# Moving the tile rows of a two-block transformer kernel to follow the weight buffers in SBUF

## The chip, the core and the metric

The kernel runs on one core of one Trainium2 chip. The metric is the device time of one execution in microseconds. The kernel before was timed three times: 1530.94, 1524.48 and 1525.96 us, median 1525.96 us. A separate profiled execution took 1528.67 us, of which 1527.4 us lie between its first and its last instruction (its span).

## What is computed

Two blocks run one after the other on a sequence of 512 tokens of width 1024, all in float32.

```python
h = rms_norm(x, g_mix);  proj = h @ w_in          # first block: LRU branch, pooling branch, gates
x = x + (gates_a * (lru(proj) @ p_a) + gates_b * (pool(proj) @ p_b)) @ w_out
h = rms_norm(x, g_ffn)
x = x + (gelu(conv(h @ w_up)[:2816]) * conv(h @ w_up)[2816:]) @ w_down
# second block: modulation by c, SSM branch, top-k attention branch, gates, gated FFN
u = rms_norm(x) * (1 + scale1) + shift1;  z = u @ w_in_2
x = x + gate1 * ((sig(ga) * s5(z) + sig(gb) * dsa(z)) @ w_out_2)
x = x + gate2 * ((silu(u2 @ w_ffn_gate_2) * (u2 @ w_ffn_up_2)) @ w_ffn_down_2)
```

## The kernel before

Activations lie transposed: a tile is 128 channels (partitions) by S = 512 tokens, one row of 2048 bytes in each partition. Every dense product is made of 1976 blocks of 128 by 128 weights. `block` (L678) issues three matmuls of 512 columns per block: the rounded weights `whi` with the rounded activation ("hi"), the weights' rest `wlo` with "hi" (L687, L688), and `whi` with the activation's rest "lo" (L690). All three stream a tile row as the moving operand in the type float32r (the name `pl_r` in the profile); the weights are the stationary operand. That makes 3 x 1976 = 5928 such matmuls.

The weights come in units of eight blocks (4096 bytes per partition). SyncE's queue loads a unit into one of four `raw` buffers (L2375), ScalarE rounds it into one of four `whi` buffers (L1117) and writes its negative rounding into `wlo` (L1126), and a DMA from GpSimd's queue adds `raw` to that (L2259); eight units are done by VectorE instead (L2193). VectorE and ScalarE also evacuate the PSUM banks and make the "hi" and "lo" tiles (L1527, L1146 and others).

Buffers are placed once, by `Kit.__init__`. Named tensors are allocated one after the other from the first free byte of a partition, each rounded up to 32 bytes; after them `self.base` is rounded up to 32, and all other tiles are rows of 2048 bytes numbered from there. `layout` (L308) hands the row numbers out by a list of free rows, so which tile has which row number depends on the number of rows, `self.slots`, and on nothing else of the placement. `place` (L275) turns a row number into an address: `base + 2048 * i`, under two names, `pl_f` (float32) and `pl_r` (float32r).

The first free byte is 16481 and the end 229368. The kernel before has this placement in each partition (bytes; the last columns are the start's remainder):

| what | start | mod 2048 | mod 256 | mod 128 |
|---|---|---|---|---|
| `raw`, 4 x 4096 | 16512 | 128 | 128 | 0 |
| `whi`, 4 x 4096 | 32896 | 128 | 128 | 0 |
| `wlo`, 4 x 4096 | 49280 | 128 | 128 | 0 |
| `vec` (1936) | 65664 | 128 | 128 | 0 |
| `cst` (1536) | 67616 | 32 | 32 | 32 |
| `sml` (4244) | 69152 | 1568 | 32 | 32 |
| rows, 76 x 2048 | 73408 | 1728 | 192 | 64 |

(229368 - 73408) / 2048 gives 76 rows, and `layout` uses all of them.

`vec` holds the small parameter vectors, `cst` the identity, a tile of ones and a triangle, `sml` small columns that the kernel works out. Most operands of the vector work start at a row's start. Some don't: the pooling branch (L1653, L1656, L1658) works on parts of a four-row tile at 0, 2400 and 4800 bytes from its start; in the kernel before these parts start at 64, 32 and 0 modulo 128.

Of the kernel before, what the change touches and what calls it, by code (L numbers as in the profile page):

```python
# [12 lines left out]
S = 512  # L13
# [10 lines left out]
NEG = -3.0e38  # L24
BIG = 1.0e30
NBANK = 8

VECS = [
    ("g_mix", 8), ("b_gate", 16), ("conv_a_w", 40), ("conv_a_b", 10),
# [71 lines left out]
class Book:  # L101
# [5 lines left out]
    def __init__(self):  # L107
        self.events, self.gone, self.home, self.before, self.real = {}, {}, {}, {}, False
# [100 lines left out]
class Kit:  # L209


    def __init__(self, nc, top, x_d, w_d, mod_d, cond_d, vec_d, cst_d, inv_d, ssm_d, uk_d, spill_d,
                 tab_d, stk_d, xs_d, out_d):
        self.nc = nc
        self.x_d, self.w_d, self.mod_d, self.vec_d, self.cst_d, self.inv_d = (
            x_d, w_d, mod_d, vec_d, cst_d, inv_d)
        self.cond_d, self.xs_d, self.stk_d = cond_d, xs_d, stk_d
        self.ssm_d, self.uk_d, self.spill_d, self.tab_d, self.out_d = (
            ssm_d, uk_d, spill_d, tab_d, out_d)
        self.plan = []  # L220
        self.book = book = Book()
        self.at, self.freed = book.at, book.freed

        def sig(name, by=1):
            s = Sig(book, top.enter_context(nc.semaphore(name)), by)
            self.sigs.append(s)
            return s

        self.sigs = []

        self.pe_done, self.act_done = sig("pe_done"), sig("act_done")
        self.dve_done, self.pool_done = sig("dve_done"), sig("pool_done")

        self.w_hi, self.w_neg = sig("w_hi"), sig("w_neg")
        self.w_lo = [sig(f"w_lo{i}", 16) for i in range(NLO)]

        self.raw_in = [sig(f"raw_in{i}", 16) for i in range(NRAW)]
        self.mod_in = [sig(f"mod_in{i}", 16) for i in range(NMB + NMC)]
        self.x_out = [sig(f"x_out{i}", 16) for i in range(8)]
        self.x_in = [sig(f"x_in{i}", 16) for i in range(8)]  # L240
        self.cond_in = sig("cond_in", 16)
        self.vec_in, self.ident_in, self.tri_in, self.inv_in = (
            sig(n, 16) for n in ("vec_in", "ident_in", "tri_in", "inv_in"))
        self.ssm_in, self.uk_in, self.ki_in = (sig(n, 16) for n in ("ssm_in", "uk_in", "ki_in"))
        self.st_out = [sig(f"st_out{i}", 16) for i in range(4)]
        self.st_in = [sig(f"st_in{i}", 16) for i in range(4)]
        self.tab_out = {n: sig(f"{n}_out", 16) for n in TABS}
        self.tab_in = [sig(f"tab_in{q}", 16) for q in range(4)]
        self.gate_io = [sig(f"gate_io{i}", 16) for i in range(16)]
        self.y_out = [sig(f"y_out{i}", 16) for i in range(2)]  # L250

        def sb(name, shape, dt=F32):
            return top.enter_context(nc.sbuf_tensor(name, shape, dt))

        self.banks = [top.enter_context(nc.psum_tensor(f"ps{i}", [128, S], F32))[:, :]
                      for i in range(NBANK)]
        self.raw = sb("raw", [128, NRAW, UB * 128])
        self.whi = sb("whi", [128, NHI, UB * 128], F32R)
        self.wlo = sb("wlo", [128, NLO, UB * 128], F32R)
        self.vec = sb("vec", [128, NV])  # L260
        self.cst = sb("cst", [128, 3, 128])
        self.sml = sb("sml", [128, NSML])
        self.ident, self.ones, self.tri = (self.cst[:, i, :] for i in range(3))
        self.base = (nc.sbuf_base + 31) // 32 * 32
        self.slots = (nc.sbuf_usable_end - self.base) // (4 * S)
        self.made = {}
        self.bank = {}

# [387 lines left out]
def tensor_engine(k, T):  # L656
# [4 lines left out]
    matmul, transpose = T.eng.matmul, T.eng.transpose  # L661
    free = [(i, None) for i in range(NBANK)]
    ready = set()
# [2071 lines left out]
```

## Time and profile before

| | |
|---|---|
| three timed runs | 1524.48, 1525.96, 1530.94 us |
| profiled execution | 1528.67 us |
| its span | 1527.4 us |
| TensorE busy / VectorE / ScalarE / GpSimd | 98% / 48% / 56% / 16% of the span |
| mean granted TensorE clock | 0.990 |
| matmuls in all, of them float32r of 512 columns | 7256, 5928 |

The profile gives each instruction with its line, its engine and its tiles. A matmul's shown duration (390 ns) is longer than the distance from one matmul's start to the next one's, since they are pipelined; where it matters here, the distance between starts is read from a list of instructions in order of time.

### The profile page before, as it was taken

The numbers are of one execution on the slowest core, as the hardware profiler recorded it, in microseconds if no ns is written. First come the engines' busy times: TensorE is split into PE (matmuls) and PEld (weight loads), VectorE is DVE, ScalarE is ACT, GpSimd is POOL, SyncE is SP. The second block draws the span as 40 slices with busy tenths as digits, with TensorE's granted clock in tenths as the row PEclk, the third lists the DMA queues.
The fourth block names the chain that finished last, engine by engine and source line by source line (L and its number), as shares of the span: only waits on it lengthen the run. The fifth ranks groups of instructions, "written<-read, shape, count | busy, mean of one in ns | idle before, by whom it ended". The sixth has DMA issues, their size and how long they took to land.

```text
span 1527.4 us, 18719 instructions
## 1 busy us (share of the span) xinstructions
PE 1492.1 (98%) x7256; PEld 1207.9 (79%) x7256; DVE 732.5 (48%) x1373; ACT 854.1 (56%) x1099; POOL 248.8 (16%) x275
## 2 busy tenths in 40 slices
PE   9999999999999999999997999999999999999998
PEld 7877888887878888888876777876878888888886
DVE  5788643555596958443134457925663212110011
ACT  6778876935565546554443575488345444444441
POOL 1111111111111111111112431121011111111111
PEclk9999999999999999999998999999999999999999
DMA  9777887799999798799879867986587998888882
GB/s 263 186 172 169 198 181 187 184 304 304 294 252 272 206 223 218 186 272 232 212 200 290 242 154 187 211 249 216 153 205 186 236 233 194 192 190 196 188 184 83
DMA packets 98648, 324.71 MB, mean 213 GB/s; under 512 B 10992, under 2 KB 13040, under 8 KB 98432
## 3 DMA queue, kind: packets, MB, share of 16 engines
q0 software_dynamic: 34400, 125.17, 44.2%
q1 hardware_dynamic: 60624, 191.39, 37.1%
q10 hardware_dynamic: 3536, 6.95, 1.2%
q8 instruction: 58, 0.95, 0.2%
q14 instruction: 30, 0.25, 0.0%
HBM read 179.69 MB, written 18.87 MB: 130 GB/s over the span
## 4 chain that ended last, share of the span: by engine, by line
PE 80%; DMA 8%; DVE 6%; ACT 4%; issue 1%; SPq 1%; POOL 0%; ACTq 0%; DVEq 0%
PE ps L687 25%; PE ps L688 25%; PE ps L690 24%; DMA wlo<-raw 3%; DMA raw<-in_w 2%; DVE pl_f L1914 1%; DMA pl_f<-stk 1%; ACT whi L1117 1%; ACT wlo L1126 1%; DMA tab<-pl_f 1%; PE ps L731 1%; DVE pl_r L1527 1%; PE ps L1011 1%; PE ps L1031 1%; DMA pl_f<-tab 1%
## 5 line engine op out<-in xcount | busy, mean ns | idle before, releaser
L687 PE MATMUL ps<-pl_r,whi 128*128 128x512 f32 x1976 | 783.3, 396 | 10.7 <-DMA wlo<-raw 5.6
L688 PE MATMUL ps<-pl_r,wlo 128*128 128x512 f32 x1976 | 775.3, 392 | 0.0
L690 PE MATMUL ps<-pl_r,whi 128*128 128x512 f32 x1976 | 774.2, 392 | 0.0
L687 PEld LDWEIGHTS ps<-pl_r,whi 128*128 128x128 f32 x1976 | 372.5, 189 | 101.9 <-issue 15.2
L690 PEld LDWEIGHTS ps<-pl_r,whi 128*128 128x128 f32 x1976 | 372.0, 188 | 84.7 <-DVE pl_r L1544 0.9
L688 PEld LDWEIGHTS ps<-pl_r,wlo 128*128 128x128 f32 x1976 | 372.6, 189 | 78.0 <-issue 0.5
L2259 POOL DMA_DIRECT2D wlo<-raw x238 | 203.8, 858 | 1173.2 <-ACT wlo L1126 1145.7
L1117 ACT ACTIVATE whi<-raw 128x1024 fp32r<-128x1024 f32 x247 | 259.9, 1053 | 184.8 <-PE ps L690 132.5
L1126 ACT ACTIVATE wlo<-raw 128x1024 fp32r<-128x1024 f32 x238 | 248.8, 1045 | 0.0
L1527 DVE TENSOR_TENSOR pl_r<-pl_f,pl_r 128x512 fp32r<-128x512 f32 x116 | 80.3, 692 | 44.7 <-ACT pl_r L1146 28.3
L2231 DVE TENSOR_TENSOR pl_f<-ps,pl_f 128x512 f32<-128x512 f32 x22 | 15.2, 691 | 172.9 <-PE ps L690 172.9
L1146 ACT ACTIVATE pl_r<-pl_f 128x512 fp32r<-128x512 f32 x38 | 24.0, 631 | 99.9 <-DVE pl_f L2231 77.7
L1283 ACT ACTIVATE pl_f<-ps,vec 128x512 f32<-128x512 f32 x44 | 33.9, 775 | 63.7 <-PE ps L690 60.0
L2208 DVE SCALAR_TENSOR_TENSOR pl_f<-ps,sml,pl_f 128x512 f32<-128x512 f32 x16 | 12.0, 749 | 117.8 <-PE ps L690 117.8
L1136 ACT ACTIVATE pl_f<-pl_f 128x512 f32<-128x512 f32 x38 | 23.8, 628 | 71.4 <-DVE pl_f L2208 51.3
L1914 DVE CUSTOM_DVE_ANT_0 pl_f<-pl_f,pl_f 128x1024 f32<-128x1024 f32 x48 | 57.9, 1217 | 2.1 <-DMA pl_f<-in_mod 2.1
L2001 DVE TENSOR_TENSOR pl_f<-pl_f,ps 128x512 f32<-128x512 f32 x8 | 5.5, 687 | 73.9 <-PE ps L690 73.9
L1968 DVE SCALAR_TENSOR_TENSOR pl_f<-ps,vec,pl_f 128x511 f32<-128x511 f32 x44 | 32.8, 745 | 14.7 <-ACT pl_f L1283 14.7
L1480 ACT ACTIVATE pl_f<-ps 128x512 f32<-128x512 f32 x22 | 13.1, 596 | 42.8 <-PE ps L690 42.7
L1971 DVE SCALAR_TENSOR_TENSOR pl_f<-ps,vec,pl_f 128x511 f32<-128x511 f32 x44 | 33.0, 750 | 1.6
L1855 DVE TENSOR_TENSOR pl_f<-pl_f,sml 128x640 f32<-128x640 f32 x4 | 3.3, 824 | 57.8 <-DMA tab<-pl_f 57.8
L1614 DVE SCALAR_TENSOR_TENSOR pl_f<-ps,vec,pl_f 128x511 f32<-128x511 f32 (+1 forms) x30 | 22.4, 748 | 16.8 <-ACT pl_f L1204 16.1
(263 smaller groups left out, 1089.4 us busy)
## 6 DMA issues: line engine op xcount, KB each, us to landing
raw<-in_w SPq DMA_DIRECT2D x245, 512.0 KB, 5.3
wlo<-raw POOLq DMA_DIRECT2D x238, 512.0 KB, 6.2
pl_f<-in_mod SPq DMA_DIRECT2D x48, 512.0 KB, 9.5
pl_f<-tab SPq DMA_DIRECT2D x12, 512.0 KB, 8.0
xs<-pl_f SPq DMA_DIRECT2D x16, 256.0 KB, 7.2
tab<-pl_f SPq DMA_DIRECT2D x8, 512.0 KB, 5.8
pl_f<-xs SPq DMA_DIRECT2D x16, 256.0 KB, 5.2
spill<-pl_f ACTq DMA_DIRECT2D x16, 256.0 KB, 4.8
```

The lines of the kernel that those rows point to most:

```text
L687: matmul(out, wh, sr(pair, kk, "hi"), start=start, stop=False)
L688: matmul(out, wl, sr(pair, kk, "hi"), start=False, stop=False)
L690: mm = matmul(out, wh, sr(pair, kk, "lo"), start=False, stop=stop)
L1117: act(k.whi[:, u % NHI, :], k.raw[:, u % NRAW, :], ACT.Copy).then_inc(*k.w_hi.tick(("w_hi", u)))
L1126: act(k.wlo[:, u % NLO, :], k.raw[:, u % NRAW, :], ACT.Copy, scale=-1.0).then_inc(*k.w_neg.tick(("w_neg", u)))
L1146: act(sr(pair, m, "hi"), src, ACT.Copy).then_inc(*done.tick((pair, m, "hi")))
L1283: act(sb("up", j), ps("w_up", j), ACT.Identity, bias=vc("conv_f_b", j), scale=vc("conv_f_w", 44 + j)).then_inc(*done.tick(("up_tap", j)))
L1527: tt(sr(pair, m, "lo"), src, sr(pair, m, "hi").bitcast(F32), ALU.subtract).then_inc(*done.tick((pair, m, "lo"), *freed_by))
L1914: V.eng.tensor_tensor_reduce(r, r, sb(*c), 1.0, 0.0, ALU.mult, ALU.add, sm("mod", u)).then_inc(*done.tick(("mod_used", u), *([mod_home(u)] ...
L1968: stt(f[:, 1:S], b[:, 0:S - 1], vc("conv_f_w", j), f[:, 1:S], ALU.mult, ALU.add).then_inc(*done.tick())
L1971: stt(f[:, 0:S - 1], b[:, 1:S], vc("conv_f_w", 88 + j), f[:, 0:S - 1], ALU.mult, ALU.add).then_inc(*done.tick(("up", j), ("w_up", j)))
L2259: P.eng.dma_start(k.wlo[:, u % NLO, :].bitcast(F32), k.raw[:, u % NRAW, :], accum_op=ALU.add).then_inc(*k.w_lo[u % NLO].tick(("w_lo", u)))
```

## The change

A constant `NSLOT = 76` is added. The rows' base is taken right behind `wlo`, one tensor `slots` of 76 rows is allocated there to keep the place, and `vec`, `cst` and `sml` are allocated behind it.

```diff
 NBANK = 8
+NSLOT = 76
@@
         self.wlo = sb("wlo", [128, NLO, UB * 128], F32R)
+        self.base = (nc.sbuf_base + 31) // 32 * 32
+        self.slots = NSLOT
+        sb("slots", [128, NSLOT * S])
         self.vec = sb("vec", [128, NV])
         self.cst = sb("cst", [128, 3, 128])
         self.sml = sb("sml", [128, NSML])
         self.ident, self.ones, self.tri = (self.cst[:, i, :] for i in range(3))
-        self.base = (nc.sbuf_base + 31) // 32 * 32
-        self.slots = (nc.sbuf_usable_end - self.base) // (4 * S)
         self.made = {}
```

By the same arithmetic the rows then start at 65664 (128 modulo 2048, 128 modulo 256, 0 modulo 128), 7744 bytes lower. `vec` starts at 221312, `cst` at 223264 and `sml` at 224800, each 155648 = 76 x 2048 bytes higher, so with the remainders of before; `sml` ends at 229044. `raw`, `whi` and `wlo` stay. Row numbers, instructions, their order, waits and sizes are the same.

## Rows read from the trace of the kernel before

**Rows 1.** The page: span, busy engines, slices of granted clock

```profile
span 1527.4 us, 18719 instructions
PE 1492.1 (98%) x7256; PEld 1207.9 (79%) x7256; DVE 732.5 (48%) x1373; ACT 854.1 (56%) x1099; POOL 248.8 (16%) x275
PEclk9999999999999999999998999999999999999999
```

**Rows 2.** The page's costliest groups: line, operation, count | busy, mean ns | idle before

```profile
L687 PE MATMUL ps<-pl_r,whi 128*128 128x512 f32 x1976 | 783.3, 396 | 10.7 <-DMA wlo<-raw 5.6
L688 PE MATMUL ps<-pl_r,wlo 128*128 128x512 f32 x1976 | 775.3, 392 | 0.0
L690 PE MATMUL ps<-pl_r,whi 128*128 128x512 f32 x1976 | 774.2, 392 | 0.0
```

**Rows 3.** Waits of TensorE: engine, line, releaser: us in total, times, longest

```profile
PE ps L900 <- DMA pl_f<-stk: 8.7, 1, 8.7
PE ps L687 <- DMA wlo<-raw: 5.6, 4, 2.9
PE ps L687 <- DVE pl_f L1614: 3.0, 1, 3.0
...
PE ps L900 <- DMA pl_f<-tab: 1.5, 1, 1.5
```

**Rows 4.** TensorE in order of time, the end of the last product: start, duration, line

```profile
1507.44 0.39 PE L687 MATMUL ps<-pl_r,whi 128*128 128x512 f32 x1
...
1513.16 0.39 PE L688 MATMUL ps<-pl_r,wlo 128*128 128x512 f32 x1
1513.39 0.39 PE L690 MATMUL ps<-pl_r,whi 128*128 128x512 f32 x1
```

**Rows 5.** The same list, TensorE between 100 and 102.5 us

```profile
100.15 0.63 PE L687 MATMUL ps<-pl_r,whi 128*128 128x512 f32 x1
...
102.29 0.63 PE L690 MATMUL ps<-pl_r,whi 128*128 128x512 f32 x1
```

**Rows 6.** Busy time by stretch: PE, PEld, DVE, ACT, POOL (count), clock, DMA share, GB/s

```profile
100.00:102.50 2.50, 2.50 (x7) 1.92 (x7) 2.40 (x4) 1.70 (x2) 0.51 (x1) 0.50 0.91 210
1200.00:1300.00 100.00, 100.00 (x438) 82.05 (x438) 21.59 (x34) 45.20 (x54) 15.86 (x19) 1.00 0.90 218
1507.40:1513.40 6.00, 6.00 (x28) 4.89 (x28) 0.00 (x0) 0.00 (x0) 0.00 (x0) 1.00 0.00 0
```

**Rows 7.** TensorE around a plain float32 product from rows (two instructions each)

```profile
928.40 0.39 PE L690 MATMUL ps<-pl_r,whi 128*128 128x512 f32 x1
928.63 3.60 PE L972 MATMUL ps<-pl_f,pl_f 128*128 128x512 f32 x8
```

**Rows 8.** Durations by line, ns min/median/max: weight loads from `cst`, from rows, from `whi`

```profile
L764 PEld LDWEIGHTS ps<-cst x52: 192/192/338, 1.1 to 8.1; 128*128 128x128 f32 x52
L972 PEld LDWEIGHTS ps<-pl_f,pl_f x8: 188/190/190, 928.4 to 931.2; 128*128 128x128 f32 x8
L690 PEld LDWEIGHTS ps<-pl_r,whi x1976: 186/188/334, 19.4 to 1514.8; 128*128 128x128 f32 x198
```

**Rows 9.** Durations by line, VectorE operands at remainders 0, 32 and 64 of 128

```profile
L1656 DVE TENSOR_TENSOR pl_f<-pl_f,pl_f x8: 691/692/694, 45.5 to 129.6; 128x512 f32<-128x512 f32 x8
L1527 DVE TENSOR_TENSOR pl_r<-pl_f,pl_r x116: 691/692/694, 18.7 to 1395.1; 128x512 fp32r<-128x512 f32 x116
```

**Rows 10.** Durations by line, ScalarE: at a row's start, shifted, and between `raw` and `whi`

```profile
L1480 ACT ACTIVATE pl_f<-ps x22: 580/597/599, 1171.9 to 1388.2; 128x512 f32<-128x512 f32 x22
L1198 ACT ACTIVATE pl_f<-ps x8: 597/598/600, 44.2 to 126.1; 128x512 f32<-128x512 f32 x8
L1117 ACT ACTIVATE whi<-raw x247: 1040/1052/1081, 13.2 to 1492.6; 128x1024 fp32r<-128x1024 f32 x124
```

**Rows 11.** Groups of ScalarE: a copy of 512 columns from row to row

```profile
L1146 ACT ACTIVATE pl_r<-pl_f 128x512 fp32r<-128x512 f32 x38 | 24.0, 631 | 99.9 <-DVE pl_f L2231 77.7 <-DVE pl_f L2167 18.2 <-DVE pl_f L2153 3.8
```

## Prediction

> **What bounds the kernel now.** I read the page first: TensorE is busy for 1492.1 of 1527.4 us, while VectorE, ScalarE and GpSimd stand at 48%, 56% and 16% [rows 1]. The costliest groups are the three float32r matmuls of `block`, 1976 of each, with 10.7 us of idle time ahead of them in all [rows 2]. The waits confirm it: the longest are 8.7, 5.6 and 3.0 us in total [rows 3]. So the end is set by TensorE's own pace and hardly by anything that it waits for.
>
> The pace has to be read from starts. In the last product 26 distances lie between 1507.44 and 1513.39 us: 5.95 / 26 = 0.2288 us each [rows 4], at the full granted clock, 2.4 GHz, with no other engine busy and no DMA running (third line of [rows 6]). In the middle of the second FFN, with VectorE at 22%, ScalarE at 45% and the DMA engines at 90%, 438 matmuls lie in 100 us, which is the same pace (the first and last of them are cut by the window's edges) (second line of [rows 6]). The 5928 matmuls at 0.2288 us are 1356 us, 89% of the span. This is the only quantity by which an edit that adds and removes nothing could move the time much, so the question is what the 228.8 ns are made of and whether an address is among it.
>
> 512 columns at 2.4 GHz are 213.3 ns. 15.5 ns per matmul are over. In a stretch at the lower level, 1.2 GHz, five distances between 100.15 and 102.29 us are 0.428 us each [rows 5, 6], and 512 / 1.2 is 426.7 ns: there nothing is over, within the 10 ns to which the list is rounded. So the surplus shows only where the array takes a column in 0.42 ns. The plain float32 product L972, whose operands lie in the same rows, takes (3.60 - 0.59) / 7 = 0.430 us per instruction, 0.59 being the one matmul's duration [rows 7]; that is 1024 array cycles (426.7 ns), with 3 ns over. It streams its 512 columns at half the pace and has no surplus of 15 ns either. The surplus thus belongs to streaming four bytes per partition and array cycle. What causes it (a cost of that type, or of where the operand starts) the trace can't say, since every float32r moving operand before starts at 64 modulo 128.
>
> **The change part by part.** No instruction, wait, semaphore, DMA or row number is removed, added or moved. What changes are operands' addresses: the rows by -7744 bytes, the small tensors by +155648.
>
> *The small tensors* keep their remainders modulo 2048; I cost them at nothing. They are read as scale and bias columns and in some of the 7256 - 5928 = 1328 other matmuls [rows 1, 2]; 3 ns on each of these would be 4 us, which I keep as the bound on either side.
>
> *Weight loads* read `whi` and `wlo`, which stay. Even where loads differ in place the time doesn't: 192 ns from `cst` (32 modulo 128), 190 from rows (64), 188 from `whi` (0) [rows 8]. Zero.
>
> *VectorE.* The pooling line L1656 has the first operand and the result of four of its eight instructions at 32 modulo 128 and of the other four at 0, and all eight lie between 691 and 694 ns; L1527, at 64, has the same 691 to 694 [rows 9]. After the change L1527 is at 0, which is already among the cases seen. Zero, from a direct comparison.
>
> *ScalarE.* L1198 writes at 4 to 32 bytes into its tile and takes 598 ns; L1480, at row starts, takes 597 [rows 10]. The copy from `raw` to `whi`, both at 0 modulo 128, takes 1052 ns for 1024 columns; the copy between rows, at 64, takes 631 for 512 [rows 10, 11]. The difference, 421 ns for 512 columns, leaves 210 ns of fixed part in either, so no extra shows for the 64. Zero, and 5 ns either way on some 500 such instructions would lie beside TensorE's work, since ScalarE has 44% idle.
>
> *DMAs* into and out of rows move 2048 or 4096 bytes per partition. Those that end a wait of TensorE are 8.7 + 5.6 + 1.5 = 15.8 us together [rows 3]; of these 5.6 us belong to `wlo`<-`raw`, whose addresses stay. Of the other 10.2 us a transfer whose length changed by 5% would give or take 0.5 us (an estimate from those rows). Bounds -1 to +1 us, taken as 0.
>
> *The moving operand of the 5928 matmuls* is the one unknown. Within the trace its cost doesn't depend on which row is read (rows follow one another by 2048 bytes, and the pace is the same in every stretch above), nor on the distance between it and the weight columns: weights start at 128, 640, 1152 and 1664 modulo 2048, the rows at 1728, and no period of four appears in the starts (all 26 distances of the stretch of rows 4 are 0.22 or 0.23 us). Its bounds are: below, the whole surplus gone, 5928 x 15.5 = 92 us less; above, one more surplus on a quarter of them (the second rival), 23 us more. I take 0, because each operation whose address could be compared, on three engines, showed none, and because L972, which reads its moving operand from the same rows, has almost no surplus.
>
> Sum: 1528.67 + 0 = 1528.67 us for the profiled execution. That execution lies 2.7 us over the median of the timed runs; against the median the forecast is 1526 us. Its own range is the spread of the timed runs, 1524.5 to 1530.9, with 1 us of DMA and 4 us for the small tensors on either side: 1519 to 1535.
>
> **Rivals.** *First: the surplus is the price of the start at 64 modulo 128.* If the moving operand is read in pieces of 128 bytes, a row of 2048 that starts in the middle of a piece needs 17 of them and one that starts at a piece's edge needs 16. A piece is 32 columns, 13.3 ns at 2.4 GHz; 228.8 - 13.3 = 215.5, which would leave 2.2 ns over, near the 3 ns over that L972 has. For it speaks that this fits to within a nanosecond, that the surplus is absent where the array takes columns at half the pace (a supply with reserve hides the extra piece), and that the change makes just this remainder 0. Against it: one fit of one number; a start at 64 is as good as one at 0 for the vector engines; and a cost of float32r itself would look the same. Price: some 5900 matmuls at the full clock x 13.3 ns = 78 us, so 1526 - 78 = 1448 us; other work has room for it (ScalarE 56% and VectorE 48% busy), but the DMA engines, 90% busy in the second FFN, may give 10 to 20 us back as waits for weights, 1448 to 1468 us. By the Trainium skill's page "TensorE: Matmul & The Clock Gate", section "Wait — 56ns, not 53.3ns?", matmuls that follow one another start N / 2.4 ns plus about 2.5 ns apart, at N = 512 215.7 ns; the trace disagrees (228.8), the page's figure is for another type, and if it held here once the rows are moved, the time would be this rival's. "SBUF — State Buffer", section "Who interferes with whom", says that TensorE never waits for another engine's access, with which the equal pace beside idle and busy engines agrees [rows 6].
>
> *Second: the rows now have the weights' remainder, 128 modulo 2048.* The next matmul's weights are loaded while the present one streams, and in every fourth block both reads then start at the same remainder, where before they never did. If the two ports met in the same part of the memory there, a quarter of the matmuls, 1482, would be held. At one more surplus each, 15.5 ns, that is 23 us: 1549 us. It decides from 5.1 ns on (7.6 us / 1482). Against it: ScalarE's copy from `raw` to `whi` reads and writes at equal remainders and lies on the same straight line as the copy between rows [rows 10, 11] (though there one is a read and the other a write). For it: nothing but that it is new.
>
> *Third: the addresses don't do what the diff says,* for instance because the rows' number changed and `layout` gave other rows. 76 x 2048 from 65664 ends at 221312 and `sml` at 229044, under 229368, so it fits, and the number is the one of before. This is counted with "no change".
>
> **How the numbers follow.** No effect: 0.63, 1526 us. First rival: 0.25 (0.17 for all of it, 0.08 for a part). Second rival, or another loss of its kind: 0.12. Half a percent, 7.6 us, is about what a measurement of this kernel can tell from no change. Of the 0.63, 0.02 may fall on either side of it by chance: same 0.59, faster 0.27, slower 0.14. The range must leave out no more than 2 in 10. Without the first rival it would leave out a quarter; with it and without the second it leaves out about 0.15. So it reaches from 1446 to 1535; the likeliest case alone is 1519 to 1535.
>
> **What would show it.** With no effect the starts in the last product stay 0.2288 us apart, the count in a window of 100 us of the second FFN stays at 438, and the durations of L1527, L1656 and L1480 stay at 692, 692 and 597 ns. By the first rival the distance is 0.2155 us and the count some 465, and new waits for `wlo`<-`raw` appear. By the second, one block in four has distances over 0.24 us and the others 0.2288. The prediction is wrong if the pace of float32r matmuls moves by more than 7.6 us / 5928 = 1.3 ns.

## Result and the profile after

The changed kernel takes 1519.04 us (median of 9 runs, 1517.28 to 1523.24) against 1525.96 us of the kernel before in the same comparison: ratio 0.995, 95% interval 0.9936 to 0.9964. It is 6.9 us faster. The profiled execution took 1518.45 us, 10.2 us less than the one of before.

The page of the changed kernel, its lines of span and engines and the three matmul groups (line numbers are 2 higher, so L689, L690 and L692 are L687, L688 and L690 of before):

```profile
span 1517.2 us, 18719 instructions
PE 1481.3 (98%) x7256; PEld 1208.2 (80%) x7256; DVE 733.0 (48%) x1373; ACT 854.1 (56%) x1099; POOL 248.9 (16%) x275
...
L689 PE MATMUL ps<-pl_r,whi 128*128 128x512 f32 x1976 | 777.4, 393 | 12.4 <-DMA wlo<-raw 7.3
L692 PE MATMUL ps<-pl_r,whi 128*128 128x512 f32 x1976 | 771.3, 390 | 0.0
L690 PE MATMUL ps<-pl_r,wlo 128*128 128x512 f32 x1976 | 770.9, 390 | 0.0
```

Against [rows 1] VectorE, ScalarE and GpSimd are busy for the same time to 0.5 us, and TensorE for 10.8 us less. Against [rows 2] the same matmuls show 2 to 3 ns less each. The time went from TensorE's own pace. TensorE in order of time in the last product of the changed kernel:

```profile
1497.27 0.39 PE L689 MATMUL ps<-pl_r,whi 128*128 128x512 f32 x1
...
1502.94 0.39 PE L690 MATMUL ps<-pl_r,wlo 128*128 128x512 f32 x1
1503.16 0.39 PE L692 MATMUL ps<-pl_r,whi 128*128 128x512 f32 x1
```

Here 26 distances are 5.89 us, 0.2265 us each, where [rows 4] had 0.2288. Over long undisturbed stretches the starts give 226.7 ns (272 cycles of 1.2 GHz) after and 228.9 ns before; this is called the settled distance below. The longest waits of TensorE in the changed kernel:

```profile
PE ps L902 <- DMA pl_f<-stk: 9.0, 1, 9.0
PE ps L689 <- DMA wlo<-raw: 7.3, 4, 3.5
PE ps L689 <- DVE pl_f L1616: 3.3, 1, 3.3
```

Against [rows 3] these three are 2.3 us longer, others are shorter: the whole of the span in which TensorE is not busy is 35.9 us (1517.2 less 1481.3) against 35.3 us (1527.4 less 1492.1). Waiting has hardly changed.

### The profile page after: what moved, and what is told of

It reads as the page before. It is cut to its first block, busy times and chain, and to the rows that moved or that the text cites. A ratio compares the mean times of both kernels' runs of the same rounds, so it can differ in the third digit from the quotient of the medians.

```text
span 1517.2 us, 18719 instructions
## 1 busy us (share of the span) xinstructions
PE 1481.3 (98%) x7256; PEld 1208.2 (80%) x7256; DVE 733.0 (48%) x1373; ACT 854.1 (56%) x1099; POOL 248.9 (16%) x275
## 4 chain that ended last, share of the span: by engine, by line
PE 81%; DVE 6%; DMA 6%; ACT 5%; issue 1%; SPq 0%; POOL 0%; ACTq 0%; DVEq 0%
PE ps L689 25%; PE ps L692 25%; PE ps L690 25%; DMA wlo<-raw 2%; ACT whi L1119 1%; DMA raw<-in_w 1%; DMA pl_f<-stk 1%; DVE pl_f L1916 1%; ACT wlo L1128 1%; DVE pl_r L1529 1%; PE ps L733 1%; PE ps L1013 1%; PE ps L775 1%; PE ps L1033 1%; DMA pl_f<-tab 1%
## 5 line engine op out<-in xcount | busy, mean ns | idle before, releaser
L689 PE MATMUL ps<-pl_r,whi 128*128 128x512 f32 x1976 | 777.4, 393 | 12.4 <-DMA wlo<-raw 7.3
L692 PE MATMUL ps<-pl_r,whi 128*128 128x512 f32 x1976 | 771.3, 390 | 0.0
L690 PE MATMUL ps<-pl_r,wlo 128*128 128x512 f32 x1976 | 770.9, 390 | 0.0
L689 PEld LDWEIGHTS ps<-pl_r,whi 128*128 128x128 f32 x1976 | 372.2, 188 | 100.5 <-issue 17.7
L692 PEld LDWEIGHTS ps<-pl_r,whi 128*128 128x128 f32 x1976 | 371.9, 188 | 79.3 <-DVE pl_r L1546 0.9
L690 PEld LDWEIGHTS ps<-pl_r,wlo 128*128 128x128 f32 x1976 | 372.0, 188 | 75.9 <-issue 0.5
L1128 ACT ACTIVATE wlo<-raw 128x1024 fp32r<-128x1024 f32 x238 | 248.8, 1046 | 0.0
L1629 DVE SCALAR_TENSOR_TENSOR pl_f<-pl_f,pl_f 128x512 f32<-128x512 f32 x20 | 12.9, 689 | 36.4 <-ACT pl_f L1225 36.4
```

The lines of the kernel that those rows point to most:

```text
L689: matmul(out, wh, sr(pair, kk, "hi"), start=start, stop=False)
L690: matmul(out, wl, sr(pair, kk, "hi"), start=False, stop=False)
L692: mm = matmul(out, wh, sr(pair, kk, "lo"), start=False, stop=stop)
L1128: act(k.wlo[:, u % NLO, :], k.raw[:, u % NRAW, :], ACT.Copy, scale=-1.0).then_inc(*k.w_neg.tick(("w_neg", u)))
```

## Experiments

All of them change only where buffers lie (by unused bytes put in between), except for three that are named and two that repeat an execution. One number is compared: the mean distance between starts of float32r matmuls of 512 columns at the full clock. For most kernels a line of busy time in the stretch from 1300 to 1400 us (second FFN, nothing but such matmuls on TensorE) is shown: the first count is TensorE's matmuls in 100 us, two of which are cut by the edges. 443 stands for 226.7 ns, 439 or 438 for 228.9, 431 or 430 for 233.3. Other stretches of a kernel can differ, which is said where they do. For the two kernels of the case, before and after, in this order:

```profile
1300.00:1400.00 100.00, 100.00 (x439) 82.05 (x438) 12.52 (x19) 45.98 (x55) 15.49 (x18) 1.00 0.84 192
```

```profile
1300.00:1400.00 100.00, 100.00 (x443) 82.81 (x442) 11.53 (x18) 45.09 (x53) 16.38 (x19) 1.00 0.85 195
```

The times of kernels run once are single executions; beside them the kernel before took 1523.5 (first four), 1525.0 (next four) and 1525.7 us (the four after these).

**Which address counts?** The theories have letters, which the expectations use. First theory (A): the rows' own start modulo 128, as the prediction's first rival had it, with a smaller price. Second (B): the rows' distance from the weights' buffers (rows' start less weights' start). Third (C): the small tensors' place.

*after_64*, the changed kernel with the rows 64 bytes higher:

```diff
+        sb("pad_r", [128, 16])
         self.base = (nc.sbuf_base + 31) // 32 * 32
```

> The changed kernel with 64 unused bytes ahead of the rows: rows start at 65728 (64 modulo 128, 192 modulo 2048), the small tensors 64 bytes higher too; the weights stay (0 modulo 128). Theory A (the pace of the float32r matmuls hangs on the rows' own start modulo 128): the distance between starts in the last product goes back from 226.7 to 228.9 ns, and the time from 1519 to about 1526 to 1529 us. Theory B (it hangs on rows and weight buffers having equal remainders): 228.9 ns too. Theory C (the small tensors' place behind the rows did it): stays 226.7 ns, 1519 us.

```profile
1300.00:1400.00 100.00, 100.00 (x438) 82.05 (x438) 12.53 (x19) 45.57 (x55) 15.94 (x19) 1.00 0.83 191
```

228.9 ns and 1530.97 us. The small tensors still lie behind the rows, which speaks against theory C, though they moved by 64 bytes too (before_192, below, settles it); A and B both stand.

*before_64*, the kernel before with the same line ahead of its `self.base`: rows at 0 modulo 128, small tensors untouched.

> The kernel before with 64 unused bytes behind the small tensors, so that the rows start at 73472 (0 modulo 128, 1792 modulo 2048) and everything else stays where it was. Theory A (rows' own start modulo 128): 226.7 ns between starts and 1516 to 1521 us. Theory B (equal remainders of rows and weights modulo 2048): stays 228.9 ns, 1526 us. Theory C (place of the small tensors): 228.9 ns.

```profile
1300.00:1400.00 100.00, 100.00 (x430) 80.44 (x429) 12.46 (x18) 45.17 (x54) 15.36 (x18) 1.00 0.82 189
```

233.3 ns and 1543.82 us: neither value that was expected. Rows at 0 modulo 128, which A called good, are here worse than at 64. A has fallen, and B had only called this "as before".

*both_64*, the changed kernel with weights' buffers and rows 64 bytes higher together:

```diff
+        sb("pad_w", [128, 16])
         self.raw = sb("raw", [128, NRAW, UB * 128])
```

> The changed kernel with 64 unused bytes ahead of the raw buffers, so that weight buffers and rows all start at 64 modulo 128 and still have equal remainders (192 modulo 2048). Theory A: 228.9 ns and about 1526 us. Theory B: 226.7 ns, 1519 us. If the weights' own start counts as well, the distance is longer than 228.9 ns.

```profile
1300.00:1400.00 100.00, 100.00 (x443) 82.81 (x442) 11.90 (x18) 45.07 (x54) 16.22 (x19) 1.00 0.86 195
```

226.7 ns and 1517.15 us. Rows and weights start at 64 modulo 128 and the pace is the good one. This is what B says and A excludes. Against after_64 the rows lie at the same address, and so do the small tensors; only the weights' buffers have moved, and the distance went from 228.9 to 226.7 ns.

*weights_64*, both lines: weights at 192 modulo 256, rows at 0, a distance of 64.

> The changed kernel with 64 unused bytes ahead of the raw buffers and 64 more ahead of the rows: the weight buffers start at 64 modulo 128, the rows at 65792, which is 0 modulo 128 and modulo 256. Theory A (rows alone): 226.7 ns, 1519 us. Theory B (equal remainders): 228.9 ns. If a stationary operand at 64 modulo 128 costs by itself, over 226.7 ns; if rows at 0 modulo 256 are better than at 128, under 226.7 ns.

Two stretches of this kernel, 200 to 300 and 1300 to 1400 us:

```profile
200.00:300.00 100.00, 100.00 (x439) 82.06 (x438) 42.87 (x62) 81.48 (x98) 14.81 (x19) 1.00 0.78 186
1300.00:1400.00 100.00, 100.00 (x430) 81.00 (x429) 12.18 (x18) 44.66 (x54) 15.48 (x18) 1.00 0.83 188
```

1536.49 us, and one kernel with two paces: 233.3 ns up to about 100 us, 228.9 from there to about 1140 us, 233.3 from there to the end. Modulo 256 the addresses don't change on the way. So the pace isn't a sum of costs of single operands. It looks like a rhythm into which the stream falls and in which it mostly stays. Where it changes can be seen in the list in order of time:

```profile
93.19 0.40 PE L694 MATMUL ps<-pl_r,whi 128*128 128x512 f32 x1
...
96.69 0.39 PE L694 MATMUL ps<-pl_r,whi 128*128 128x512 f32 x1
98.91 0.47 PE L691 MATMUL ps<-pl_r,whi 128*128 128x512 f32 x1 [1.83 <-DMA wlo<-raw]
...
102.25 0.63 PE L692 MATMUL ps<-pl_r,wlo 128*128 128x512 f32 x1
102.68 0.63 PE L694 MATMUL ps<-pl_r,whi 128*128 128x512 f32 x1
...
106.55 0.39 PE L694 MATMUL ps<-pl_r,whi 128*128 128x512 f32 x1
...
109.98 0.39 PE L694 MATMUL ps<-pl_r,whi 128*128 128x512 f32 x1
```

Up to 96.69 us 15 distances are 3.50 us (233.3 ns). Then TensorE waits 1.83 us, runs at the lower clock (0.43 us apart) and, back at the full clock, 15 distances are 3.43 us (228.7 ns). The second change lies between 1140 and 1152 us, where the norm ahead of the second FFN interrupts the stream.

It isn't the only kernel that does this. after_64, at 228.9 ns elsewhere, ran at 233.3 ns from about 503 to 550 us; a line of busy time within that stretch (133 matmuls would stand for 228.9 ns here):

```profile
515.00:545.00 30.00, 30.00 (x130) 24.32 (x129) 27.70 (x50) 17.23 (x21) 5.09 (x6) 1.00 1.03 266
```

And before_64 has 233.3 ns in the stretch from 1300 to 1400 us and in some others, but 232.3 to 232.4 ns in most of those before 1160 us.

**By distance.** The changed kernel with 256, 192, 224, 96 and 32 bytes ahead of the rows (the first diff with 64, 48, 56, 24 and 8 columns).

> The changed kernel with 256 unused bytes ahead of the rows: the distance from the weight buffers to the rows is 256 modulo 512 and modulo 2048, and 0 modulo 256 and modulo 128. The runs so far give 226.7 ns between starts at a distance of 0, 228.9 at 64 and 233.3 at 128 (modulo 512). Theory D256 (only the distance modulo 256 counts): 226.7 ns, about 1518 us. Theory D512 (a longer period): another value than 226.7, most likely over 228.9 ns and 1526 us.

> The changed kernel with 192 unused bytes ahead of the rows: distance 192 modulo 512 and 256. If the cost grows with the distance (0, 64, 128: 226.7, 228.9, 233.3 ns), it is 236 ns or more, 1555 us or more. If the distance counts by its size modulo 256, as 64 on the other side of 0, it is about 228.9 ns, 1526 us. If 128 is a special bad value, anything under 233 ns.

> The changed kernel with 32 unused bytes ahead of the rows: distance 32 modulo 512. If the cost goes up evenly from 0 to 64: between 226.7 and 228.9 ns, about 1522 us. If it goes in steps of 64: one of these two. If the rows' own start at 32 modulo 64 costs by itself: over 228.9 ns.

> The changed kernel with 224 unused bytes ahead of the rows: distance 224 modulo 256, which is -32. If the cost is symmetric about 0 it is the 233.3 ns of distance 32, 1546 us. If it hangs on how long the moving operand's reads take to meet the weight load's, any other value; every value above 226.7 keeps 0 as the best place.

> The changed kernel with 96 unused bytes ahead of the rows: distance 96 modulo 256. Distances 32, 128 and 192 gave 233.3 ns, 64 gave 228.9 and 0 gave 226.7. If odd multiples of 32 are all bad: 233.3 ns and 1545 us; if the cost goes evenly from 64 to 128: about 231 ns and 1536 us.

after_256 and after_192, in this order:

```profile
1300.00:1400.00 100.00, 100.00 (x443) 82.84 (x442) 11.85 (x18) 46.72 (x55) 16.05 (x19) 1.00 0.85 195
```

```profile
1300.00:1400.00 100.00, 100.00 (x431) 80.55 (x430) 13.49 (x20) 44.48 (x53) 15.52 (x18) 1.00 0.82 188
```

| distance weights to rows, modulo 256 | kernels | ns between starts, 1300 to 1400 us | time of one execution, us |
|---|---|---|---|
| 0 | after, both_64, after_256, before_192 | 226.7 | 1518.5, 1517.2, 1520.1, 1518.5 |
| 32 | after_32 | 233.3 | 1546.3 |
| 64 | before, after_64 | 228.9 | 1528.7, 1531.0 |
| 64 | weights_64 | 233.3 (228.9 from 100 to 1140 us) | 1536.5 |
| 96 | after_96 | 233.3 | 1547.1 |
| 128 | before_64 | 233.3 | 1543.8 |
| 192 | after_192 | 233.3 | 1547.8 |
| 224 | after_224 | 233.3 | 1545.0 |

A distance of 256 is as good as 0, one of 128 is not. No even growth with the distance shows, and no symmetry: 192 should have been as good as 64 for that. 0 is good, 64 is in between, and the five others that were tried (160 was not) share the value that seems to be the ordinary one. In after_32, after_96 and after_224 the rows' own start is an odd multiple of 32 as well, and no run moves the weights along with it, so there the distance and the rows' own start aren't told apart. The kernel before owed 4.4 ns per matmul to a lucky 64, and the change made it a lucky 0.

**Which load?** *wlo_128* puts `wlo` alone at a distance of 128 (128 unused bytes ahead of `wlo` and 128 ahead of the rows).

> The changed kernel with 128 unused bytes between whi and wlo and 128 more ahead of the rows: the rows are 256 (0 modulo 256) from whi and 128 modulo 256 from wlo. Theory R (what counts is the distance between a moving operand and the stationary operand that is loaded while it streams): one of three weight loads is badly placed, so the mean distance between starts lies between the 226.7 ns of distance 0 and the 233.3 ns of distance 128, about 228.9 ns, and the time near 1526 us. Theory L (the matmul's own stationary and moving operand have to fit, or one of the buffers alone decides): likewise one third, but the long distance lies one matmul later. If the pace is set by the worst of the three: 233.3 ns, 1544 us.

TensorE in order of time (L691 is `whi` with "hi", L692 `wlo` with "hi", L694 `whi` with "lo"):

```profile
1300.29 0.40 PE L691 MATMUL ps<-pl_r,whi 128*128 128x512 f32 x1
1300.52 0.40 PE L692 MATMUL ps<-pl_r,wlo 128*128 128x512 f32 x1
1300.76 0.39 PE L694 MATMUL ps<-pl_r,whi 128*128 128x512 f32 x1
1300.98 0.40 PE L691 MATMUL ps<-pl_r,whi 128*128 128x512 f32 x1
```

From 1300 to 1400 us the mean distances are 232.4 ns from L691 to L692, 234.3 from L692 to L694, and 226.7 from L694 to the next L691. Together that is 231.1 ns per matmul, more than the 228.9 that both theories gave, and the kernel takes 1533.12 us. Theory R put the long distance where `wlo` is loaded (the first), theory L one matmul later (the second); it is both. Only where neither the matmul's own weights nor the next ones are badly placed is the distance the short one. The rows and `whi` lie here exactly as in after_256, which has 226.7 ns in all three places, so the stationary operand's place takes part, and not only the rows'. Unequal distances by themselves would not show it. The kernel before has them too, with all its buffers placed alike: 229.1, 231.7 and 225.9 ns from 1300 to 1400 us. But there the short one wanders: it stands behind L690 in that stretch and behind L687 at 1100 us. In wlo_128 it stands behind L694 nearly throughout (not in the first stream and not for some 10 us at 1046 us).

**Is the surplus the loads' reads?** Two kernels take a part of them away, at distance 0, and leave out a part of the product with them. *half_wlo*:

```diff
-        matmul(out, wl, sr(pair, kk, "hi"), start=False, stop=False)
+        matmul(out[0:64, :], wl[:, 0:64], sr(pair, kk, "hi"), start=False, stop=False)
```

> The changed kernel (distance 0), with the second of a block's three matmuls on half of the weights' columns only: its stationary operand is 128x64 instead of 128x128 (this leaves out part of the product). Its moving operand is the same 512 columns. Theory R (the surplus over 213.3 ns comes from the weight load's reads, which run beside the moving operand's): the load of these 64 columns runs while the first matmul streams, so the distance from the first to the second matmul's start (L689 to L690) falls by about 4 to 7 ns, to 220 to 223, and the two others stay at 226.7. Theory F (a fixed cost per float32r matmul, the address only adds to it): all three stay at 226.7 ns.

*narrow_b*, all matmuls but the first and last of a group on 32 weight columns:

> The changed kernel with all float32r matmuls but the first and last of a bank's group on 32 of the 128 weight columns only (this leaves out most of the product); moving operands, their number and addresses stay. Theory R (the surplus over 213.3 ns comes from the weight loads' reads beside the stream): with a quarter of these reads the distance inside a group falls from 226.7 to about 216 to 220 ns, the time to about 1460 to 1485 us. Theory F (a fixed cost of each float32r matmul, to which a bad address adds): it stays at 226.7 ns or over, as half of the columns in one of three matmuls gave 229.8.

narrow_b, weight loads by shape (busy, mean ns), and the stretch:

```profile
L691 PEld LDWEIGHTS ps<-pl_r,wlo 128*32 128x32 f32 x1976 | 215.2, 109 | 218.2 <-issue 1.7
L690 PEld LDWEIGHTS ps<-pl_r,whi 128*32 128x32 f32 x1706 | 186.1, 109 | 207.5 <-issue 2.9
```

```profile
1300.00:1400.00 100.00, 100.00 (x434) 49.86 (x433) 12.55 (x19) 45.39 (x55) 15.52 (x18) 1.00 0.83 188
```

The narrow loads take 109 instead of 188 ns, and the distance is 231 ns (230 in half_wlo): longer than with full loads, 1533.77 and 1533.85 us. So the 13.3 ns over the 213.3 ns of the columns alone don't shrink with the amount that the loads read. Theory R, as these two expectations put it, has fallen. Changing the loads' length spoils the good rhythm as an offset does.

**A map within one run.** *probe_a* adds groups of 20 matmuls at the end of the changed kernel, of the form

```python
    for i in range(20):
        o = 128 * (i % 7) + 0
        mm = matmul(b[0:128, 0:448], k.whi[:, 2, o:o + 128], x[:, 16:464], start=True, stop=True)
```

> The changed kernel with 30 groups of 20 float32r matmuls each appended at its end, into a PSUM bank that nobody reads, so that one run gives the distance between starts by the moving operand's place. Groups 1 to 16: 448 columns, moving start shifted by 0, 16, 32, ... 240 bytes against the weights' buffer. Then 512, 384 and 256 columns at shift 0 and 504, 384 and 256 at shift 32; 448 columns with 64 and 32 weight columns at shifts 0 and 32; both operands shifted by 32 and by 128 bytes; the weights alone shifted by 64 bytes; the weights alternately at 0 and 128 bytes. Theory D256 (the distance modulo 256 between moving and stationary operand): at 448 columns (186.7 ns at 2.4 GHz) shift 0 is the shortest, 200 ns if 13.3 ns of surplus stay, 64 is about 202, the others some 207 ns, and both shifted alike gives 200 again. Theory S (it is the start of one moving operand against the end of the one before, so the number of columns counts as much as the start): other column counts show another pattern, and the two operands' joint shift doesn't restore the short distance. If the surplus is a fixed number of cycles it is the same 13.3 or 20 ns at 512, 384 and 256 columns; if it is a rate, it falls in proportion.

TensorE in order of time; a group's distance is the next group's start less its own, by 20. L1121, L1130, L1133 and L1139 are 448 columns shifted by 64, 112, 128 and 160 bytes, L1157 512 columns at 0, L1178 448 columns at 0 with 32 weight columns:

```profile
1525.63 4.17 PE L1121 MATMUL ps<-pl_r,whi 128*128 128x448 f32 x20
1529.64 4.22 PE L1124 MATMUL ps<-pl_r,whi 128*128 128x448 f32 x20
...
1537.80 4.29 PE L1130 MATMUL ps<-pl_r,whi 128*128 128x448 f32 x20
1541.94 4.23 PE L1133 MATMUL ps<-pl_r,whi 128*128 128x448 f32 x20
1546.00 4.29 PE L1136 MATMUL ps<-pl_r,whi 128*128 128x448 f32 x20
1550.13 4.17 PE L1139 MATMUL ps<-pl_r,whi 128*128 128x448 f32 x20
1554.14 4.25 PE L1142 MATMUL ps<-pl_r,whi 128*128 128x448 f32 x20
...
1574.48 4.72 PE L1157 MATMUL ps<-pl_r,whi 128*128 128x512 f32 x20
1579.05 3.65 PE L1160 MATMUL ps<-pl_r,whi 128*128 128x384 f32 x20
...
1599.31 4.20 PE L1178 MATMUL ps<-pl_r,whi 128*32 128x448 f32 x20
1603.35 4.27 PE L1181 MATMUL ps<-pl_r,whi 128*64 128x448 f32 x20
```

At 448 columns (186.7 ns of stream) shifts of 16, 64 and 160 bytes give 200 ns, 112 and 144 give 207, and the others lie between. Shift 0, which should have been the shortest, gives 207 in its first group and settles at 203. Both operands shifted by 32 bytes together settle at 203 like shift 0, but both shifted by 128 bytes together at 207: here the distance alone doesn't decide. At 512 columns and shift 0 the settled distance is 226.7 again. So the rule "distance 0 modulo 256 is the good one" holds for streams of 512 columns and not for 448: the number of columns counts as well. That fits theory S in part (that it is the end of a stream which counts isn't shown); D256 has fallen as a general rule. Common to all groups of 384 columns and more is the bound: the surplus settles between 13.3 and 20 ns (16 and 24 cycles of 1.2 GHz), whatever the place, the number of columns and the width of the loads. At 256 columns and a shift of 32 bytes it is 10 ns. The best case of this kernel, 226.7 ns, is at the lower end, and no address tried goes under it.

**The change's other half, and the time.** *before_192* is the kernel before with 192 unused bytes ahead of the rows: distance 0 modulo 256, the small tensors where they were.

> The kernel before with 192 unused bytes between the small tensors and the rows: the small tensors stay ahead of the rows, the rows start at 73600, 1792 bytes above the remainder of the weights' buffers, which is 0 modulo 256. Theory D256 (the place of the rows against the weights' buffers modulo 256 is all that the change did): 226.7 ns between starts, 1518 to 1520 us, ratio to the kernel before 0.995. Theory C (moving the small tensors behind the rows is a part of it): less than that gain.

```profile
1300.00:1400.00 100.00, 100.00 (x443) 82.81 (x442) 11.51 (x18) 45.09 (x53) 16.34 (x19) 1.00 0.85 196
```

226.7 ns, 1519.51 us (median of 12) against 1527.42 (17 runs): ratio 0.9938, interval 0.9915 to 0.9961. It is the changed kernel's gain, without moving the small tensors, and theory C is out.

*before_again* and *after_again* are second executions.

> The kernel before once more, for the pace of a second execution. If the pace is a property of the addresses: 228.9 ns between starts in every stretch again. If an execution can settle in another pace: another value in some stretch, which would explain why the timed difference (6.9 us) is under 5900 x 2.2 = 13 us.

> The changed kernel once more: 226.7 ns in every stretch and 1517 to 1523 us if the pace is a property of the addresses.

In the same stretch TensorE has 439 matmuls in before_again and 443 in after_again, the values of the first executions; the times are 1526.72 and 1521.01 us. The pace came out the same in both executions of either kernel. Between executions something else varies by some microseconds: before_again has a mean granted clock of 0.992 and a span of 1525.4 us, where the first had 0.990 and 1527.4.

## Why the prediction was wrong, step by step

It forecast no effect, 1526 us; the kernel is 6.9 us faster. That 1519.04 us lies at the very edge of the range of the likeliest case (1519 to 1535) is luck: that edge was reached by allowing 4 us for the small tensors and 1 us for DMAs, and neither is what moved the time.

- *What bounds the kernel*: right. TensorE's pace of float32r matmuls is the only quantity that moved, and the criterion of the text (a change by more than 1.3 ns per matmul) is met by 2.2 ns.
- *Small tensors, weight loads, VectorE, ScalarE, DMA costed at nothing*: right. Busy times of VectorE and ScalarE are the same to 0.5 us, that of the weight loads is 1208.2 against 1207.9 us, and before_192 has the whole gain without the small tensors' move.
- *The moving operand costed at nothing*: this step failed; its term was 0 and measured 2.2 ns less on each settled matmul. It argued that the pace doesn't depend on the distance between rows and weight columns, since the weight columns start at 128, 640, 1152 and 1664 modulo 2048 and no period of four appears. But these four are 512 bytes apart, and what counts has a period of 256: against the rows at 1728 all four are at 64 modulo 256. The comparison could not have seen the effect. The same holds for the rows themselves, 2048 bytes apart. That an address-free pace is seen in every stretch showed only that all operands in it were alike modulo 256. Nor were its 26 distances equal: rounding to 0.22 and 0.23 us hid three that repeat, 226, 229 and 232 ns.
- *L972 as a second reason* (the same rows, with 3 ns over): it argued from a stream at half the pace, and both of L972's operands lie in the rows, so that no move of the rows changes their distance. Its instructions start 429 ns apart in before, after, after_32, after_96, after_192 and before_64 alike, whatever happens to the float32r matmuls; that row bore on another case. (The 0.59 us that the text subtracts is in the trace, but not in [rows 7].)
- *First rival* (a start at 64 modulo 128 costs an extra piece, 1448 us): the sign was right, the mechanism wrong, as before_64 and both_64 show, and the size per matmul six times too large (13.3 against 2.2 ns). The numeric fit within a nanosecond was a coincidence: the 13.3 ns are still there after the change. The Trainium skill's page "TensorE: Matmul & The Clock Gate", section "Wait — 56ns, not 53.3ns?", gives 215.7 ns for 512 columns; no run here settles under 226.7 ns with float32r, so that figure doesn't hold for this type.
- *Second rival* (equal remainders of rows and weights, 1549 us): it named the quantity that counts, the rows' place against the weights', and had its sign wrong. Equal remainders are the best case and not a new collision, and since modulo 256 all weight columns are alike, they are met by every matmul and not by a quarter.
- *The sum*: a settled 2.2 ns on 5928 matmuls would be 13.2 us. The traces have 5783 such distances at the full clock in either kernel; their mean is 228.98 ns before and 226.97 after, 2.0 ns apart, which is 11.6 us. The changed kernel needs a while to settle after each interruption: between 1000 and 1050 us its mean is 229.3 ns, where before had 229.7. Everything else in TensorE's time (waits, other matmuls, stretches at the lower clock) took 1.4 us more, which leaves the 10.2 us between the two profiled executions. In the pair before_again and after_again these are 9.6 us less and 3.9 more. What gives this part back isn't resolved by the runs. The timed difference, 6.9 us (7.9 for before_192), is smaller than 10.2 because the profiled execution of before was 2.7 us slower than its median and the one of after 0.6 us faster.

What stays open is why the stream falls into these rhythms. From 1300 to 1400 us the sums of three distances are 680, 686.7, 693.3 (wlo_128) and 700 ns in the kernels with full loads, or 816, 824, 832 and 840 cycles of 1.2 GHz, each a multiple of 8, as if starts were held to a coarse grid. The 232.3 ns of before_64 in other stretches (697 ns for three) don't fit this. No run tests it.

## What to carry to other kernels

Where a kernel is bound by back-to-back float32r matmuls, read the distance between their starts and try the start of the moving operands against that of the stationary ones in steps of 32 bytes, over 256: here the worst and the best differ by 6.7 ns in 227 per matmul, 3%, and by some 30 us in 1518, 2% of the time, for nothing but unused bytes. A new small buffer in front of them can cost as much: 32 bytes made 1546.3 us of 1518.5 (after_32). Which distance is best has to be tried for the number of columns at hand, since at 448 it was another than at 512. And before a row is taken as evidence that an address doesn't matter, work out by what the addresses in it differ: steps of 512 bytes say nothing on a period of 256.

## What was not expected of the hardware

- The distance of float32r matmuls of 512 columns at 2.4 GHz settles at 226.7, 228.9 or 233.3 ns (213.3 for the columns alone), by the distance of the operands modulo 256, and at 232.3 in about half of before_64; at 1.2 GHz it is some 427 ns in all of them, with nothing over.
- One kernel (weights_64) ran at 228.9 ns for some 1040 us and at 233.3 ns before and after, with no change of addresses modulo 256; another (after_64) at 233.3 ns for some 45 us and at 228.9 otherwise.
- Shorter weight loads (109 instead of 188 ns) made the matmuls no denser: 231 instead of 226.7 ns between starts.
